# Two token tiles of a fp32 transformer kernel run one after the other across each norm

## The chip, the cores and the metric

The kernel runs on one core of a Trainium2 chip. The metric is the device time of one execution in microseconds (us). One profiled execution gives the trace from which every row below is taken.

## What is computed

Two two-layer blocks follow each other on 256 tokens of width 1024, all in float32. Only the row of operations matters here:

```
for l in 0, 1:   x = x + gate1 * attention(modulate(rmsnorm(x)))      # 88 weight units
                 x = x + gate2 * (relu(h @ w_ff1)^2 @ w_ff2)          # h = modulate(rmsnorm(x)), 64 units
x = rmsnorm(x)
x = layer_norm(ALPHA * x + retention(x))
x = layer_norm(ALPHA * x + swiglu(x))
x = layer_norm(ALPHA * x + sparse_attention(x))
x = layer_norm(ALPHA * x + mixture_of_8_experts(x))
```

Seven norms stand between two stages of matrix products (four RMS norms after the first one, and three layer norms); one more stands before the first product and one after the last.

## The kernel before

**Tiles and units.** The 256 tokens are two tiles of 128 (`NT`). Weights stream through the core in units of 512 KB (128 partitions x 1024 values: two row blocks of 512 columns, or four of 256). For each unit SyncE starts a DMA into `raw` (ring of 4), ScalarE copies it rounded into `whi` (L1175), VectorE writes the rest into `wlo` (L1635), and TensorE multiplies: `unit` (L432) runs both token tiles over one unit, high part with high and low part of the tokens (L440), then the low part of the weights (L446). `whi` and `wlo` are rings of 4, and ScalarE and VectorE split three units ahead (`LEAD`); a slot is free again when `unit_used` has been raised by the last product of its unit. Every unit is 24 products of 128 x 256 or 12 of 128 x 352 or 128 x 512.

**Order.** Each engine's program is written out by hand and waits on counted semaphores. `chunk` and `side_chunk` are four units that sum into one pair of PSUM banks; `side_chunk` leaves the reading of the banks to `c.pending`, which runs after the next split. `pass_units(e, n)` on ScalarE and VectorE is n splits. `c.weave` hangs side work on a unit number.

**Around a norm.** TensorE finishes the last unit of both tiles; VectorE reads the sums out of PSUM and adds them to `x` (L2073 and L2076 after attention, L2089 and L2100 after the MLP, L2160 after retention and SwiGLU, L2331 after sparse attention); the norm's statistics are squares on ScalarE (L1266) or `bn_stats` on VectorE (L2129), then a root on ScalarE (L1257, L1269); VectorE writes the normed tiles (L1776, L2145 and L2148), and drains (L1747, `to_pe`) to release TensorE. TensorE turns tile 0 and tile 1 (`turn_tiles`, L471), eight 128 x 128 blocks each, ScalarE copies each bank of four into `xh` (L1229), VectorE the rest into `xl` (L1714). Only when all four banks are done do the units of the next stage begin. In the MLPs `clear_sums` (L789) stands before them.

## Time and profile before

| | |
|---|---|
| median of three runs | 3045.28 us (3038.07 to 3046.09) |
| the profiled execution | 3036.44 us |
| its span, first to last instruction | 3034.7 us |
| busy: TensorE, VectorE, ScalarE | 2702.1, 2147.5, 1611.3 us |
| mean granted TensorE clock | 0.942 of 2.4 GHz |
| chain that ended last | TensorE 80%, VectorE 8%, ScalarE 5% |
| one 512 KB weight load, issue to landing (medians by tensor) | 4.3 to 5.6 us |
| first matrix product of the experts' routing | 1948.14 us after the start |

The span is the row of stages laid end to end. The seven norms' turns start at 429.4, 643.6, 1015.8, 1226.3, 1467.9, 1684.0 and 1935.8 us. "Idle" is time of one engine before an instruction, with what ended it; PEclk is the granted clock, where 1.00 is 2.4 GHz and 0.50 is 1.2 GHz.

### The profile page before, as it was taken

The numbers are of one execution on the slowest core, as the hardware profiler recorded it, in microseconds if no ns is written. First come the engines' busy times: TensorE is split into PE (matmuls) and PEld (weight loads), VectorE is DVE, ScalarE is ACT, GpSimd is POOL, SyncE is SP. The second block draws the span as 40 slices with busy tenths as digits, with TensorE's granted clock in tenths as the row PEclk, the third lists the DMA queues.
The fourth block names the chain that finished last, engine by engine and source line by source line (L and its number), as shares of the span: only waits on it lengthen the run. The fifth ranks groups of instructions, "written<-read, shape, count | busy, mean of one in ns | idle before, by whom it ended". The sixth has DMA issues, their size and how long they took to land.

```text
span 3034.7 us, 39536 instructions
## 1 busy us (share of the span) xinstructions
PE 2702.1 (89%) x12842; PEld 2183.6 (72%) x12842; DVE 2147.5 (71%) x2585; ACT 1611.3 (53%) x2056; POOL 19.8 (1%) x37
## 2 busy tenths in 40 slices
PE   3889879987988899898899868699999999999997
PEld 2767758875766687666799646578878887888875
DVE  6666657766666565655555675489888998989998
ACT  2454534445454344333344344277767776777775
POOL 0000000000000000000000000000000000000000
PEclk9999989999999899899899868699999999999999
DMA  6636547745464465544455430299989998999995
GB/s 225 202 117 190 172 152 257 250 149 161 133 194 159 141 213 175 176 128 146 142 180 182 129 101 1 79 322 364 338 306 342 330 368 294 361 335 342 358 355 214
DMA packets 357975, 666.19 MB, mean 220 GB/s; under 512 B 23008, under 2 KB 57312, under 8 KB 357200
## 3 DMA queue, kind: packets, MB, share of 16 engines
q1 hardware_dynamic: 354080, 648.45, 63.6%
q0 software_dynamic: 3760, 15.91, 1.6%
q8 instruction: 88, 1.44, 0.2%
q14 instruction: 47, 0.39, 0.0%
HBM read 663.23 MB, written 1.05 MB: 219 GB/s over the span
## 4 chain that ended last, share of the span: by engine, by line
PE 80%; DVE 8%; ACT 5%; issue 3%; DMA 2%; DVEq 2%; ACTq 0%; SPq 0%
PE ps L440 46%; PE ps L446 23%; PE ps L482 2%; DVE wlo L1635 2%; ACT whi L1175 2%; PE ps L1078 1%; DVE mod_sum L1655 1%; DMA raw<-in_w_ada 1%; PE ps L471 1%; PE ps L581 1%; PE ps L516 1%; DMA raw<-in_w_in 1%; ACT att L1334 0%; PE ps L691 0%; DVE yl L1721 0%
## 5 line engine op out<-in xcount | busy, mean ns | idle before, releaser
L1635 DVE TENSOR_TENSOR wlo<-raw,whi 128x1024 fp32r<-128x1024 f32 x709 | 865.8, 1224 | 582.4 <-ACT whi L1175 576.1
L1175 ACT ACTIVATE whi<-raw 128x1024 fp32r<-128x1024 f32 x709 | 749.1, 1060 | 794.5 <-PE ps L446 679.0
L440 PE MATMUL ps<-whi,xh 128*128 128x512 f32 (+3 forms) x1376 | 512.2, 382 | 19.4 <-issue 6.1
L440 PE MATMUL ps<-whi,xl 128*128 128x512 f32 (+3 forms) x1376 | 496.5, 371 | 0.0
L440 PE MATMUL ps<-whi,gathered_hi 128*128 128x512 f32 x896 | 362.9, 405 | 16.9 <-issue 11.2
L440 PE MATMUL ps<-whi,gathered_lo 128*128 128x512 f32 x896 | 356.1, 397 | 0.0
L446 PE MATMUL ps<-wlo,xh 128*128 128x512 f32 (+3 forms) x1376 | 326.1, 365 | 0.0
L440 PEld LDWEIGHTS ps<-whi,xh 128*128 128x128 f32 x1376 | 270.9, 197 | 72.4 <-issue 15.4
L440 PEld LDWEIGHTS ps<-whi,xl 128*128 128x128 f32 x1376 | 271.3, 197 | 43.3 <-issue 4.0
L440 PE MATMUL ps<-whi,yh 128*128 128x512 f32 (+2 forms) x696 | 280.7, 405 | 20.8 <-DVE yl L1721 11.6
L446 PE MATMUL ps<-wlo,gathered_hi 128*128 128x512 f32 x896 | 283.1, 397 | 0.0
L440 PE MATMUL ps<-whi,yl 128*128 128x512 f32 (+2 forms) x696 | 273.8, 395 | 0.0
L446 PEld LDWEIGHTS ps<-wlo,xh 128*128 128x128 f32 x1376 | 242.0, 194 | 42.1
L1635 DVE TENSOR_TENSOR wlo<-spare,whi 128x1024 fp32r<-128x1024 f32 x168 | 204.5, 1224 | 19.0 <-ACT whi L1175 17.4
L1635 DVE TENSOR_TENSOR wlo<-mod_b,whi 128x1024 fp32r<-128x1024 f32 x168 | 205.4, 1222 | 16.2 <-ACT whi L1175 11.3
L440 PEld LDWEIGHTS ps<-whi,gathered_hi 128*128 128x128 f32 x896 | 169.7, 189 | 56.8 <-issue 16.8
L1175 ACT ACTIVATE whi<-spare 128x1024 fp32r<-128x1024 f32 x168 | 178.9, 1065 | 52.1 <-PE ps L446 52.1
L1175 ACT ACTIVATE whi<-mod_b 128x1024 fp32r<-128x1024 f32 x168 | 178.3, 1061 | 49.8 <-PE ps L446 49.5
L446 PEld LDWEIGHTS ps<-wlo,gathered_hi 128*128 128x128 f32 x896 | 169.3, 189 | 41.3
L440 PEld LDWEIGHTS ps<-whi,gathered_lo 128*128 128x128 f32 x896 | 169.8, 190 | 37.0
L446 PE MATMUL ps<-wlo,yh 128*128 128x512 f32 (+2 forms) x696 | 189.7, 393 | 5.9 <-DVE wlo L1635 5.9
L440 PE MATMUL ps<-whi,hidden_hi 128*128 128x512 f32 x448 | 178.5, 398 | 2.5 <-DVE hidden_lo L1721 1.3
(358 smaller groups left out, 3305.6 us busy)
## 6 DMA issues: line engine op xcount, KB each, us to landing
raw<-in_moe_w_in SPq DMA_DIRECT2D x227, 512.0 KB, 5.4
spare<-in_moe_w_in SPq DMA_DIRECT2D x165, 512.0 KB, 5.6
mod_b<-in_moe_w_out SPq DMA_DIRECT2D x165, 512.0 KB, 5.5
raw<-in_w_ff SPq DMA_DIRECT2D x128, 512.0 KB, 4.5
raw<-in_w_ada SPq DMA_DIRECT2D x96, 512.0 KB, 4.3
raw<-in_w_in SPq DMA_DIRECT2D x96, 512.0 KB, 4.5
work<-in_moe_w_in SPq DMA_DIRECT2D x56, 512.0 KB, 5.4
work<-in_moe_w_out SPq DMA_DIRECT2D x56, 512.0 KB, 5.2
```

What stands on the lines that cost most here:

```text
L440: e.matmul(ps[0:lhs[2], banks[t], at:at + width], part[:, k0 + j, t * P:t * P + lhs[2]], whi[:, slot, w], start=first and j == 0 and part ...
L446: mm = e.matmul(ps[0:lhs[2], banks[t], at:at + width], lhs[0][:, k0 + j, t * P:t * P + lhs[2]], wlo[:, slot, w], start=False, stop=last an ...
L471: tr = e.transpose(ps[:, bank, j * P:(j + 1) * P], src(t, b + j), ident)
L482: tr = e.transpose(ps[:, bank, (j * tiles + t) * P:(j * tiles + t + 1) * P], src(t, b + j), ident)
L516: e.matmul(ps[:, 7, :], k_("ones"), mod_sum[:, n % 2, :], start=True, stop=True).then_inc(mod_summed, 1)
L581: mm = e.matmul(ps[:, 4 + t, h * HD:(h + 1) * HD], side_pT[g][:, at:at + P], v(b, h), start=b == 0, stop=b == t)
L1078: mm = e.matmul(ps[:, bank, j * P:(j + 1) * P], part[:, t, k * P:(k + 1) * P], onehot[b][:, t, :], start=t == 0, stop=t == 1)
L1175: e.activation(whi[:, slot, :], src, ACT.Copy).then_inc(split_hi, 1)
L1635: e.tensor_tensor(wlo[:, slot, :], src, whi[:, slot, :].bitcast(F32), ALU.subtract).then_inc(split_lo, 1)
L1655: last = e.scalar_tensor_tensor(total, w[:, j, :], c_col[:, k:k + 1], total, ALU.mult, ALU.add)
```

## The change

The last four units before a norm (two after SwiGLU) and the first four units after it are run tile by tile: `by_tile` runs tile 0 through all units of the group and then tile 1, so all four ring slots hold their units until tile 1 has used them. `tile_used` tells VectorE when tile 0's columns are summed. The output units of the last MLP step and of retention are ordered by column half, and SyncE's loads with them. VectorE reads, norms and hands over tile 0, splits a unit, and then does the same for tile 1; the low-part copies of the turned tiles (`turn_first`, `turn_second`) stand among the splits. TensorE turns tile 0 before the next group and tile 1 before the group's fourth unit of tile 0. Wide operations become pieces of 512 columns of one tile. ScalarE runs a small root (`ready_root`) early, squares each tile by halves, and roots each tile by itself. `clear_sums` comes after the first four units. Side work of the modulation in the MLP moves one unit earlier, `scale_gain` two. At the kernel's start the first chunk alone is run by tile. After the sparse attention only the last four units are, since the routing follows the norm. The last layer norm is as before.

```diff
+            def half_unit(e, lhs, t, ahead, k0, bank, width, first, last, blocks=UROWS, at=0):
+
+                slot, _ = c.slot(ahead)
+                e.wait_ge(split_hi, c.at("unit", ahead + 1))
+                for j in range(blocks):
+                    w = slice(j * USIZE // blocks, j * USIZE // blocks + width)
+                    for part in lhs[:2]:
+                        e.matmul(ps[:, bank, at:at + width], part[:, k0 + j, t * P:(t + 1) * P], whi[:, slot, w],
+                                 start=first and j == 0 and part is lhs[0], stop=False)
+                e.wait_ge(split_lo, c.at("unit", ahead + RING + 1))
+                for j in range(blocks):
+                    w = slice(j * USIZE // blocks, j * USIZE // blocks + width)
+                    mm = e.matmul(ps[:, bank, at:at + width], lhs[0][:, k0 + j, t * P:(t + 1) * P], wlo[:, slot, w],
+                                  start=False, stop=last and j == blocks - 1)
+                return mm
+
+            def by_tile(e, lhs, group, between={}, tell=False):
+
+                for t in range(NT):
+                    for i, (k0, banks, width, first, last, blocks, at) in enumerate(group):
+                        for piece in between.get((t, i), ()):
+                            piece(e)
+                        mm = half_unit(e, lhs, t, i if t == 0 else 0, k0, banks[t], width, first, last, blocks, at)
+                        if t == 0:
+                            if last and tell:
+                                mm.then_inc(tile_used, 1)
+                            continue
+                        mm.then_inc(unit_used, 1)
+                        c.add("unit")
+                        for piece in c.passed():
+                            piece(e)
+
+            def tile_turns(src, t):
+
+                def piece(e):
+                    source(e)
+                    for b in range(0, KB, 4):
+                        bank = 6 + c.parity("t")
+                        e.wait_ge(t_lo, c.at("t", 1))
+                        for j in range(4):
+                            tr = e.transpose(ps[:, bank, j * P:(j + 1) * P], src(t, b + j), ident)
+                        tr.then_inc(t_ready, 1)
+                        c.add("t")
+                return piece
+
+            def from_turns(src, second):
+
+                return {(0, 0): [lambda e: e.wait_ge(t_lo, c.at("t", 1))], (0, second): [turned],
+                        (0, 3): [tile_turns(src, 1)], (1, 0): [turned]}
+
+            def first_chunk(e, src, lhs, width=UCOLS):
+
+                tile_turns(src, 0)(e)
+                side = c.parity("chunk")
+                e.wait_ge(evac_act, c.at("chunk", 1))
+                e.wait_ge(evac_dve, c.at("chunk", 1))
+                by_tile(e, lhs, [(i * UROWS, (2 * side, 2 * side + 1), width, i == 0, i == 3, UROWS, 0) for i in range(4)],
+                        from_turns(src, 2))
+                c.add("chunk")
...
+            def last_out(e, hid, kind):
+
+                n_kg = kind[0] // 256
+                by_tile(e, hid, [(kg * UROWS, (2 + 2 * n, 3 + 2 * n), UCOLS, False, kg == n_kg - 1, UROWS, 0)
+                                 for n in range(2) for kg in range(n_kg)], tell=True)
+
+            def mlp(e, src, lhs, hid, width, kind):
                 wide, _, pair, tiles = kind
                 steps = width // wide
+                tile_turns(src, 0)(e)
+                e.wait_ge(evac_act, c.at("chunk", 1))
+                e.wait_ge(evac_dve, c.at("chunk", 1))
+                if kind is SWIGLU:
+                    group = [(4 * i, (0, 1), wide, i == 0, i == 1, 4, part * wide) for part in range(2) for i in range(2)]
+                else:
+                    group = [(i * UROWS, (0, 1), UCOLS, i == 0, i == 3, UROWS, 0) for i in range(4)]
+                by_tile(e, lhs, group, from_turns(src, 1 if kind is SWIGLU else 2))
...
-                step_out(e, hid, kind, last=True)
+                last_out(e, hid, kind)
...
-                turn_tiles(e, lambda t, b: work[:, t, b * P:(b + 1) * P], KB)
-                turned(e)
-                for _ in range(3):
+                    at(ATT_UNITS - SIDE + 8 * n + 16, sum_modulation)
+
+                first_chunk(e, lambda t, b: work[:, t, b * P:(b + 1) * P], X, 352)
+                for _ in range(2):
...
-                chunk(e, Y, NT, D)
-
-                turn_tiles(e, lambda t, b: work[:, t, b * P:(b + 1) * P], KB)
-                turned(e)
-                mlp(e, X, Y, D_FF, RELU2)
+                last_chunk(e, Y)
+
+                mlp(e, lambda t, b: work[:, t, b * P:(b + 1) * P], X, Y, D_FF, RELU2)
...
+            def layer_norm_roots(e, units):
+
+                pass_units(e, 1)
+                ready_root(e)
+                for t in range(NT):
+                    vec(e)
+                    e.activation(st[:, 8 + t:9 + t], st[:, t:t + 1], ACT.Sqrt).then_inc(act_ready, 1)
+                    if t == 0:
+                        pass_units(e, units - 1)
+                        nothing_to_read(e)
+                        turn(e, xh, KB, by_tile=(0,))
...
+                def last_columns(e, t):
+                    tmp = att[:, 1024 + t * 512:1536 + t * 512]
+                    e.tensor_tensor(tmp, ps[:, 2 * side + t, :], gate1[1], ALU.mult)
+                    e.drain()
+                    if t:
+                        e.sem_inc(evac_dve, 1)
+                        e.sem_inc(bias_used[1], 1)
+                    e.tensor_tensor(x[:, t, 512:D], x[:, t, 512:D], tmp, ALU.add)
+                    to_act(e)
+                pass_units(e, 1)
+                to_act(e)
+                for t in range(NT):
+                    scaled_half(e, mod_a, t, 0)
+                tile_done(e)
+                last_columns(e, 0)
+                scaled_half(e, mod_a, 0, 1)
+                tile_inverse(e, 0)
+                shifted_tile(e, mod_a, 0)
+                pass_units(e, 1)
+                e.wait_ge(unit_used, c.at("unit", RING + 2))
+                last_columns(e, 1)
+                turn_first(e)
+                pass_units(e, 1)
+                scaled_half(e, mod_a, 1, 1)
+                tile_inverse(e, 1)
+                shifted_tile(e, mod_a, 1)
+                pass_units(e, 1)
+                c.add("chunk")
...
+            def add_columns(e, t, n, src):
+
+                w = slice(n * 512, (n + 1) * 512)
+                e.scalar_tensor_tensor(x[:, t, w], x[:, t, w], ALPHA, src, ALU.mult, ALU.add)
+                e.drain()
+                if t and n:
+                    e.sem_inc(evac_dve, 1)
+                e.bn_stats(st[:, 32 + 12 * t + 6 * n:38 + 12 * t + 6 * n], x[:, t, w])
+
+            def tile_deviation(e, t):
+
+                e.drain()
+                e.bn_aggr(st[:, 64 + 2 * t:66 + 2 * t], st[:, 32 + 12 * t:44 + 12 * t])
+                e.drain()
+                e.tensor_scalar(st[:, t:t + 1], st[:, 65 + 2 * t:66 + 2 * t], LN_EPS, None, ALU.add)
+                to_act(e)
+
+            def normed_tile(e, t):
+
+                e.scalar_tensor_tensor(x[:, t, :], x[:, t, :], st[:, 64 + 2 * t:65 + 2 * t], gain_a[:, :],
+                                       ALU.subtract, ALU.mult)
+                tile_inverse(e, t)
+                e.scalar_tensor_tensor(x[:, t, :], x[:, t, :], st[:, 16 + t:17 + t], gain_b[:, :], ALU.mult, ALU.add)
+                to_pe(e)
+
+            def layer_norm_by_tile(e, units, src, done=()):
+
+                pass_units(e, 1)
+                take_gain(e, 0)
+                take_gain(e, 1)
                 for n in range(2):
-                    if n:
-                        half_moments(e, 0)
-                    e.wait_ge(unit_used, c.at("unit", RING - 1 + n))
-                    w = slice(n * 512, (n + 1) * 512)
-                    for t in range(NT):
-                        e.scalar_tensor_tensor(x[:, t, w], x[:, t, w], ALPHA, ps[:, 2 + 2 * n + t, :], ALU.mult, ALU.add)
-                e.drain().then_inc(evac_dve, 1)
+                    if n not in done:
+                        tile_done(e)
+                        add_columns(e, 0, n, src(0, n))
+                tile_deviation(e, 0)
+                normed_tile(e, 0)
+                if 0 not in done:
+                    e.wait_ge(unit_used, c.at("unit", RING + units // 2 - 1))
+                    add_columns(e, 1, 0, src(1, 0))
+                pass_units(e, 1)
+                turn_first(e)
+                e.wait_ge(unit_used, c.at("unit", RING + units - 2))
+                add_columns(e, 1, 1, src(1, 1))
+                tile_deviation(e, 1)
+                if units > 2:
+                    pass_units(e, 1)
+                normed_tile(e, 1)
+                if units > 2:
+                    pass_units(e, 1)
+                c.add("chunk")
+                e.sem_inc(gain_a_used, 1)
+                e.sem_inc(gain_b_used, 1)
...
-            def mlp_out(e, w_out, kind, s):
-                for kg in range(kind[0] // 256):
-                    for n in range(2):
-                        (load_expert if kind is EXPERT else load)(
-                            e, rows(w_out, s * kind[0] + kg * 256)[:, :, n * 512:(n + 1) * 512])
+            def mlp_out(e, w_out, kind, s, by_columns=False):
+                order = [(kg, n) for kg in range(kind[0] // 256) for n in range(2)]
+                for kg, n in sorted(order, key=lambda o: o[::-1]) if by_columns else order:
+                    (load_expert if kind is EXPERT else load)(
...
-            for kg in range(8):
-                for n in range(2):
-                    load(sp, rows(a["ret_w_out_2"][0], kg * 256)[:, :, n * 512:(n + 1) * 512])
+            for kg, n in [(kg, n) for kg in range(6) for n in range(2)] + [(kg, n) for n in range(2) for kg in (6, 7)]:
+                load(sp, rows(a["ret_w_out_2"][0], kg * 256)[:, :, n * 512:(n + 1) * 512])
```

## Rows read from the trace of the kernel before

**Rows 1.** Waits of TensorE: us in total, times, longest.

```profile
PE ps L471 <- DVEq L1747: 69.7, 8, 11.5
PE ps L471 <- DVE xl L1714: 8.8, 8, 1.9
```

**Rows 2.** Windows over seven passages: busy (x) by engine, PEclk, DMA share, GB/s.

```profile
409.70:450.62 40.92, 30.47 (x117) 22.94 (x115) 22.73 (x24) 14.64 (x18) 1.60 (x3) 0.79 0.40 129
623.35:659.16 35.81, 24.85 (x112) 21.56 (x113) 22.96 (x24) 12.36 (x17) 0.53 (x1) 0.81 0.27 76
996.17:1037.36 41.19, 30.74 (x117) 23.13 (x115) 22.72 (x24) 14.64 (x18) 0.00 (x0) 0.79 0.30 103
1206.69:1245.79 39.10, 28.87 (x112) 22.87 (x113) 20.24 (x21) 12.35 (x17) 2.09 (x4) 0.78 0.48 164
1447.59:1491.13 43.54, 31.23 (x165) 26.57 (x163) 23.27 (x28) 12.25 (x14) 5.69 (x7) 0.76 0.43 124
1669.32:1703.99 34.67, 22.62 (x89) 17.92 (x90) 20.72 (x26) 9.23 (x12) 1.06 (x2) 0.75 0.27 85
1917.85:1948.14 30.29, 15.26 (x65) 11.98 (x64) 20.76 (x24) 10.29 (x12) 1.06 (x2) 0.76 0.16 52
```

**Rows 3.** Windows inside the first passage, same columns.

```profile
421.00:429.40 8.40, 0.02 (x1) 0.03 (x1) 6.32 (x7) 3.88 (x6) 1.60 (x3) 0.73 0.61 196
429.40:442.20 12.80, 10.73 (x32) 7.46 (x33) 5.28 (x6) 3.34 (x5) 0.00 (x0) 0.51 0.14 43
```

**Rows 4.** Timeline of TensorE, first passage: start, us, operation, [idle before].

```profile
429.38 1.97 PE L471 MATMUL ps<-const,work 128*128 128x128 f32 x8 [8.38 <-DVEq L1747]
...
437.17 0.80 PE L440 MATMUL ps<-whi,xh 128*128 128x512 f32 x1
```

**Rows 5.** Timeline of TensorE: unit pace at 352 and 256 columns; four turns.

```profile
655.36 0.32 PE L440 MATMUL ps<-whi,xh 128*128 128x352 f32 x1
...
657.26 0.32 PE L440 MATMUL ps<-whi,xh 128*128 128x352 f32 x1
...
1485.43 0.28 PE L440 MATMUL ps<-whi,xh 128*128 128x256 f32 x1
...
1488.28 0.28 PE L440 MATMUL ps<-whi,xh 128*128 128x256 f32 x1
...
1498.81 0.60 PE L482 MATMUL ps<-const,att 128*128 128x128 f32 x4
```

**Rows 6.** Timeline of VectorE, first passage.

```profile
411.05 1.23 DVE L1635 TENSOR_TENSOR wlo<-raw,whi 128x1024 fp32r<-128x1024 f32 x1 [1.56 <-ACT whi L1175]
...
421.04 1.29 DVE L2073 TENSOR_TENSOR att<-ps,mod_a 128x512 f32<-128x512 f32 x2 [0.40 <-PE ps L446]
...
428.01 2.69 DVE L1776 SCALAR_TENSOR_TENSOR work<-work,st,mod_a 128x1024 f32<-128x1024 f32 x2
431.16 0.69 DVE L1714 TENSOR_TENSOR xl<-ps,xh 128x512 fp32r<-128x512 f32 x1 [0.46 <-ACT xh L1229]
```

**Rows 7.** Timeline of ScalarE, first passage.

```profile
423.71 1.06 ACT L1266 ACTIVATE att<-x 128x1024 f32<-128x1024 f32 x1 [4.32 <-DVEq L1740]
...
430.53 0.60 ACT L1229 ACTIVATE xh<-ps 128x512 fp32r<-128x512 f32 x1 [2.80 <-PE ps L471]
```

**Rows 8.** Timeline of VectorE at the layer norm after retention.

```profile
1458.68 1.28 DVE L2160 SCALAR_TENSOR_TENSOR x<-x,ps 128x512 f32<-128x512 f32 x2
1460.05 1.29 DVE L2129 BATCH_NORM_STATS2 st<-x 128x6 f32<-128x512 f32 x2
...
1465.20 1.28 DVE L2145 SCALAR_TENSOR_TENSOR x<-x,st,gain_a 128x1024 f32<-128x1024 f32 x1 [0.16 <-issue]
```

**Rows 9.** Windows after short idles in the two attention layers.

```profile
262.00:272.00 10.00, 6.29 (x25) 4.67 (x24) 7.25 (x11) 6.19 (x13) 0.00 (x0) 0.83 0.55 168
...
848.00:858.00 10.00, 6.28 (x33) 5.17 (x34) 6.71 (x9) 7.29 (x15) 0.00 (x0) 1.00 0.66 205
```

**Rows 10.** Window over the experts' stage.

```profile
1948.14:3034.70 1086.56, 1041.04 (x4658) 834.09 (x4658) 945.75 (x989) 790.71 (x882) 0.00 (x0) 0.97 0.92 326
```

More of the change, by code:

```diff
@@ L1487, in retention @@
                 root(e, 8)
-                for half in range(2):
-                    turn(e, yh, KB)
-                    pass_units(e, 8)
-                c.add("chunk")
-                left_to_dve(e)
-                root(e, 2)
+                turn(e, yh, KB)
+                pass_units(e, 8)
+                turn(e, yh, KB)
+                pass_units(e, 4)
+                layer_norm_roots(e, 4)
             def sparse_attention(e):
-                turn(e, xh, KB, by_tile=True)
                 for i in (3, 4):
-                    chunk(e, D, copy_to(proj[:, 0, i * 512:(i + 1) * 512]))
+                    chunk(e, D, copy_to(proj[:, 0, i * 512:(i + 1) * 512]), {0: [turn_second]} if i == 3 else {})
                 def gates(e, b):
@@ L1920, in mlp @@
                 turn(e, hid[0], hid[1], kind[0] // P, kind[3])
-                pass_units(e, kind[0] // P)
-                c.add("chunk")
+                end(e)
             def layer(e, l):
@@ new lines, in from_mlp @@
+                    turn_first(e)
+                    e.wait_ge(unit_used, c.at("unit", RING + 2))
+                    columns(1, 1)
+                    pass_units(e, 1)
+                    if l + 1 < DEPTH:
+                        for n in range(2):
+                            scaled_half(e, mod_b, 1, n)
+                    normed(1)
+                    if l + 1 == DEPTH:
+                        e.sem_inc(gain_a_used, 1)
+                    pass_units(e, 1)
+                    c.add("chunk")
@@ L2112, in inverse_deviation, with tile_done @@
+                mlp(e, (yh, yl), D_FF, RELU2, from_mlp)
+            def tile_done(e):
+                c.add("tile")
+                e.wait_ge(tile_used, c.at("tile"))
             def inverse_deviation(e, n, final=False):
@@ L2229, in retention @@
                         to_pe(e)
-                for half in range(2):
-                    turn(e, yh, yl, KB)
-                    pass_units(e, 8)
-                c.add("chunk")
+                turn(e, yh, yl, KB)
+                pass_units(e, 8)
+                turn(e, yh, yl, KB)
+                pass_units(e, 4)
                 e.drain().then_inc(extra_used, 1)
-                add_mlp(e)
-                layer_norm(e)
+                layer_norm_by_tile(e, 4, mlp_sum)
             def act_copied(e):
```

298 lines of the change are left out of this document (165 added, 133 removed).

## The prediction

> **What bounds the kernel now.** I read the table of busy times and the chain first: TensorE is the engine that ends last nearly everywhere. Then TensorE's waits: the largest is not for weights but for VectorE's drain ahead of the turns at the norms, 69.7 us in 8 places, of which 11.5 us is the kernel's start, so 58.2 us in seven norms; 8.8 us more goes while the turned tiles are copied [rows 1]. Third, the windows. I cut a passage around each norm, from the first product of the last group of units before it to the last product of the first four units after it; for the seventh, to the first product of the routing [rows 2]. The six full passages last 40.9, 35.8, 41.2, 39.1, 43.5 and 34.7 us, the seventh 30.3. Their DMA share is 0.16 to 0.48, so weights are not what they wait for. Fourth, the inside of the first passage: 8.4 us with TensorE idle and VectorE busy for 6.3, and behind it 12.8 us at a granted clock of 0.51, the lower level of 1.2 GHz [rows 3]: turns, cleared sums and a first unit that starts at 437.17, 16.2 us after the last product [rows 4]. The time is lost twice, as a gap and as slow work behind it.
>
> **The floor of a passage.** A unit of 512 columns takes 2.79 us (passage one begins with four of them in 11.3 us, before the window of 8.4 us idle [rows 2, 3]); 352 columns take 1.90 and the 256-column form 2.85 [rows 5]. Four turns take about 0.45 us start to start at the full clock (0.60 with the tail [rows 5]), sixteen about 1.9. So the first passage holds 8 x 2.79 + 1.9 + 0.9 (cleared sums at the full clock) = 25.1 us of TensorE work in 40.9. I don't expect the floor: VectorE has its own chain.
>
> **The change, walked through.** Prices on VectorE: a split 1.23, a 512-column read or add 0.69 alone and 0.64 in a pair, a scaled and shifted tile 1.35, a low copy 0.69 [rows 6]; a 1024-column layer-norm pass 1.28, a statistics piece 0.69 alone [rows 8]. On ScalarE: a split 1.06, a bank of the turned tile 0.60, a 1024-column square 1.06 and so a half about 0.6 plus 0.2 to read its sum [rows 7]. A drain or a hand-off is counted at 0.1 to 0.3.
>
> First passage, microseconds from its start. TensorE runs tile 0 until 5.6 and tile 1 until 11.2, at no new cost: the same 48 products. The fourth unit's low part is ready at 2.6 and is needed at about 5. VectorE reads the earlier columns until 5.1, scales two halves until 6.4, reads and adds tile 0's last columns until 7.9, scales until 8.6; square and root end on ScalarE at 9.2; the inverse and the shifted tile are done at 11.0, before TensorE is free. Tile 0 costs TensorE nothing: its whole norm lies under tile 1's products. Then the order of VectorE decides. A split (12.2), tile 1's last columns (13.6), tile 0's two low copies (14.3, 14.9), a split (16.2), scaling, inverse and shift of tile 1 (18.5), a split (19.7), a split (20.9), then tile 1's low copies. TensorE turns tile 0 at 11.2 to 12.1, waits to 14.4, runs the half of unit one, waits 0 to 0.5 us in unit two, waits in unit three for the low part of 19.7 (about 1.6 us), turns tile 1 until 21.1, runs unit four's half until 22.5, waits 0.4 for tile 1's copies, and runs tile 1's four halves to 28.5; cleared sums bring 29.4. That is 11.5 less than 40.9.
>
> The others, in the same way. Passage two (MLP to 352-column chunk): both column halves of tile 0 are read in turn as `tile_used` rises, VectorE's fourth split comes at about 21.9, tile 1's pass starts at 24.0 and takes 3.8: 27.8 against 35.8, 8.0 less. Passage three as one: 11.8. Passage four (final RMS norm, 512 columns, no cleared sums): 28.9 against 39.1, 10.2. Passage five (layer norm, 256 columns): tile 0's two statistics pieces and two passes end at 10.7, tile 1's at 21.0, splits three and four at 22.3 and 23.5, tile 1's pass from 25.6 to 31.3, cleared sums 32.3 against 43.5: 11.2. Passage six has only two units ahead of the norm (5.6 us of cover for a chain of 8), ends at 25.9 against 34.7: 8.8. Passage seven gains only what tile 0's norm hides, since routing needs both tiles: 28.0 against 30.3, 2.3. The sum is 11.5 + 8.0 + 11.8 + 10.2 + 11.2 + 8.8 + 2.3 = 63.8 us.
>
> At nothing I count: the start (turns of tile 1 slip behind three half units, but its copies wait as long as before; bounds -1 and +1); the reordered loads (same bytes, and the DMA share in the passages leaves room [rows 2]; without that cover a load landing late would cost up to the 4.3 to 5.6 us that one load takes from issue to landing, by the table above); the modulation's sums one unit earlier, which move on TensorE and VectorE together; `ready_root`, which lies in ScalarE's wait of 4.3 us [rows 7]; the narrow pieces' extra fixed cost, already in the prices for single pieces. A slot held for both tiles is queued before the next splits on ScalarE and, behind them, on VectorE: unit five's split can start only when tile 1 has used unit one, at 24.3 in passage one, and is whole at 26.6 where TensorE asks at 28.5, so 1.9 us of slack cover it.
>
> **What the walk leaves out.** Two things. Hand-offs: the walk has some fifteen per passage and lets them overlap ideally; between 0 and 2 us a passage, I take 1, so 6 us. The clock: TensorE now has several idles of 0.4 to 2.3 us within some 12 us. Near such a cluster the trace shows both outcomes: idles of 1.4 and 2.3 us at 264 and 267 us with a granted clock of 0.83 in that window, and idles of 3.0 and 1.8 us at the same place of layer two with 1.00 [rows 9]. If it falls, tile turns and half units run at half pace. Waits for VectorE swallow part of that, the tail does not: for passage one I get about 34 instead of 29.4, so 5 us a passage, 30 in six. The bounds are 0 and 30; rows 9 are one and one, so I take half, 15.
>
> The Trainium skill, page "TensorE: Matmul & The Clock Gate", section "A second HAM failure mode: psum-queue depth-cycling", says that short idles between groups of products, if frequent enough, make the clock swing between its levels even where no single idle is long. By that rule all six passages would fall, and the sum would be lower by the other 15 us. The trace agrees in one of the two places compared.
>
> The forecast is 63.8 - 6 - 15 = 43 us. The profiled execution of 3036.4 us would become 2993.5; its run lay 9 us under the median of 3045.3, so I forecast a median of 3002 us.
>
> **The rivals.**
> Everything fits: clock held at 2.4 GHz, hand-offs hidden. Gain 64, time 2981. For it: every single idle in the walk is under 3 us, as in the window at 848 us with clock 1.00. Against it: up to 5 us of waits in some 12 us, in passage two more than 7.
> The clock falls in every passage: 63.8 - 6 - 30 = 28, time 3017. For it, and by the rule of that page: passages two and five have the most idle. Against it: the work between the idles is dense.
> No change that can be told: the tile-1 chain on VectorE is later than walked, by 7 us more in each passage, through another order of splits and copies than I read. VectorE's busy time in a passage is 20.2 to 23.3 us [rows 2], so even a chain with no overlap at all would end a passage near 23 plus a pass of 4 to 6; that is under all lengths but leaves 5 to 12. Time about 3040.
> Slower: the low clock begins at the first idle and lasts beyond the passage. Each us of products at 1.2 GHz that would have run at 2.4 loses half of it. Before, the first passage shows 12.8 us of it [rows 3]. From about 9.5 us lost per passage (57.8/6), so 19 us of unbroken low clock, the gain is gone; at 24 us of it the kernel is about 15 us slower, 3060. Against it: the clock came back within 5 us of dense work at 437.17.
> Could the experts swallow it? Their stage has a DMA share of 0.92 [rows 10], but it holds none of the changed passages, and its loads beyond the first three wait for the routing, which comes earlier with all else; it is only moved.
>
> **How the numbers follow.** Chances: forecast (a gain of 32 to 56 us) 0.55, everything fits 0.17, clock falls everywhere 0.20, no change 0.04, slower 0.04. About 0.3%, 9 us, is what a measurement of this kernel can tell from no change; faster is thus 0.93, same 0.03, slower 0.04. The range takes in both clock bounds with some us of the run-to-run spread: 2979 to 3024. Range of the likeliest alone: 2989 to 3013.
>
> **What would show it.** The wait of L471 for VectorE's drain falls from 69.7 us to under 20, nearly all of it the kernel's start. The six passages last 28 to 34 us. In them VectorE is busy without a gap of 1 us from tile 0's first read to tile 1's low copies; new waits of TensorE are for `wlo` (in the half of unit two or three) and for `xl`. Cleared sums at 0.9 us show a held clock, at 1.9 a fallen one. Wrong would be: TensorE waiting for the split of unit five (the slots), the turn of tile 0 waiting for VectorE by more than 2 us in passages one to five, or a granted clock below 0.6 over a whole new passage.

## The result: 77 us faster, 37 us more than forecast

| | before | after |
|---|---|---|
| median | 3041.76 us (3038.07 to 3046.09, 4 runs) | 2964.83 us (2963.28 to 2965.93, 4 runs) |
| profiled execution, its span | 3036.44, 3034.7 us | 2964.59, 2962.7 us |
| mean granted TensorE clock | 0.942 | 0.954 |

The ratio is 0.9744, with a 95% interval of 0.9731 to 0.9757. The forecast was 3002 us with a range of 2979 to 3024: the sign was right, and the time lies 14 us below the range.

The span shrank by 72.0 us. I cut the span after at the same places as [rows 2] and [rows 10]. Windows of the kernel after: length, busy time (and count) of TensorE, its weight loads, VectorE, ScalarE and GpSimd, then granted clock, DMA share, GB/s.

```profile
409.35:439.05 29.70, 27.15 (x117) 20.96 (x115) 22.42 (x27) 16.61 (x28) 1.61 (x3) 0.94 0.50 157
613.39:642.90 29.51, 23.88 (x112) 20.75 (x113) 20.95 (x27) 12.89 (x25) 0.00 (x0) 0.88 0.25 73
978.78:1008.84 30.06, 27.14 (x117) 20.85 (x115) 22.45 (x27) 16.62 (x28) 0.00 (x0) 0.94 0.36 121
1179.82:1208.60 28.78, 25.23 (x113) 19.60 (x114) 19.22 (x23) 12.32 (x24) 2.10 (x4) 1.00 0.48 160
1413.94:1445.79 31.85, 26.37 (x165) 22.55 (x163) 23.32 (x30) 11.93 (x16) 5.71 (x7) 1.00 0.55 150
1625.49:1652.47 26.98, 22.02 (x89) 17.22 (x89) 19.91 (x28) 9.31 (x14) 1.06 (x2) 0.87 0.33 110
1866.15:1894.39 28.24, 14.15 (x66) 11.39 (x64) 21.09 (x27) 10.36 (x14) 1.06 (x2) 0.78 0.17 57
1894.39:2962.70 1068.31, 1036.90 (x4658) 832.52 (x4658) 945.28 (x989) 790.33 (x882) 0.00 (x0) 0.98 0.93 331
```

| stretch | before, us | after, us | gain |
|---|---|---|---|
| start to the first passage | 409.70 | 409.35 | 0.35 |
| the seven passages | 265.52 | 205.12 | 60.4 |
| the six stretches between them | 1272.92 | 1279.92 | -7.0 |
| routing to the end | 1086.56 | 1068.31 | 18.25 |

Two readings. In the first passage VectorE does as much work as before (22.42 us against 22.94) and ScalarE 2 us more (16.61 against 14.64), but TensorE's share of the time rose: it is busy for 27.15 of 29.70 us, against 30.47 of 40.92, part of which was slow work. And the last row, a stage that the change doesn't touch, gave a quarter of the gain.

TensorE's waits in the kernel after (us in total, times, longest), against 69.7 and 8.8 us in [rows 1]:

```profile
PE ps L461 <- DVE xl L1833: 15.0, 13, 2.7
PE ps L494 <- DVEq L1866: 13.8, 2, 11.5
PE ps L466 <- DVE wlo L1754: 9.2, 6, 2.7
PE ps L541 <- DVEq L1866: 7.5, 1, 7.5
```

L461 and L466 are the products of half units, L494 the turns. Of the 13.8 us, 11.5 is the kernel's start; the 7.5 us is the seventh norm, where both tiles must be there. So 58.2 us of waiting for a norm became 9.8, and waits for the low copies (`xl`) and for the splits (`wlo`) are now the longer ones. TensorE in the first passage of the kernel after (start, duration, [idle before]), with `...` where lines are left out:

```profile
420.52 1.04 PE L494 MATMUL ps<-const,work 128*128 128x128 f32 x8
423.93 0.47 PE L461 MATMUL ps<-whi,xh 128*128 128x512 f32 x1 [2.38 <-DVE xl L1833]
424.24 0.39 PE L461 MATMUL ps<-whi,xl 128*128 128x512 f32 x1
...
424.80 0.63 PE L461 MATMUL ps<-whi,xl 128*128 128x512 f32 x1
...
428.35 0.40 PE L461 MATMUL ps<-whi,xh 128*128 128x512 f32 x1
...
429.74 1.03 PE L494 MATMUL ps<-const,work 128*128 128x128 f32 x8
...
432.35 0.50 PE L461 MATMUL ps<-whi,xh 128*128 128x512 f32 x1 [0.17 <-DVE xl L1833]
...
438.12 1.03 PE L859 MATMUL ps<-zero 1*128 1x512 bf16 x4
```

The turns start as the last product ends, where [rows 4] had 8.38 us of idle. The clock does fall behind the 2.38 us of idle: a 512-column product takes 0.63 in place of 0.39 us from 424.80 on. From 424.24 to 428.35 us the granted clock is 0.58, from there to the passage's end it is 1.00, and the cleared sums at 1.03 us agree. VectorE in the same passage, which the walk had laid out step by step:

```profile
415.78 0.68 DVE L2209 TENSOR_TENSOR att<-ps,mod_a 128x512 f32<-128x512 f32 x1
...
418.72 1.28 DVE L1902 SCALAR_TENSOR_TENSOR work<-work,st,mod_a 128x1024 f32<-128x1024 f32 x1
420.13 1.23 DVE L1754 TENSOR_TENSOR wlo<-raw,whi 128x1024 fp32r<-128x1024 f32 x1
...
422.98 1.29 DVE L1833 TENSOR_TENSOR xl<-ps,xh 128x512 fp32r<-128x512 f32 x2
...
426.16 1.28 DVE L1902 SCALAR_TENSOR_TENSOR work<-work,st,mod_a 128x1024 f32<-128x1024 f32 x1
427.56 2.36 DVE L1754 TENSOR_TENSOR wlo<-raw,whi 128x1024 fp32r<-128x1024 f32 x2
```

Counted from 409.35, tile 0's shifted tile ends at 10.7 us (walk: 11.0), its low copies at 14.9 (14.9), tile 1's shifted tile at 18.1 (18.5), the last two splits at 20.6 (20.9).

**Where the 18 us come from.** Behind the routing stands a loop over two experts at a time. Its body runs three times, so TensorE jumps back to its start twice. TensorE in the kernel before, at both back-jumps, and windows behind them:

```profile
2248.11 0.79 PE L440 MATMUL ps<-whi,gathered_hi 128*128 128x512 f32 x1 [3.11 <-issue]
...
2253.57 0.79 PE L440 MATMUL ps<-whi,gathered_hi 128*128 128x512 f32 x1 [4.24 <-issue]
...
2512.35 0.50 PE L440 MATMUL ps<-whi,gathered_hi 128*128 128x512 f32 x1 [2.38 <-ACT whi L1175]
...
2516.93 0.80 PE L440 MATMUL ps<-whi,gathered_hi 128*128 128x512 f32 x1 [3.85 <-issue]
```

```profile
2248.00:2266.00 18.00, 13.64 (x49) 10.53 (x50) 7.98 (x10) 6.91 (x8) 0.00 (x0) 0.73 0.55 185
2512.00:2530.00 18.00, 13.80 (x53) 10.84 (x54) 9.84 (x12) 7.29 (x9) 0.00 (x0) 0.81 0.62 207
```

TensorE stands still twice at each back-jump. In three of the four stalls it waits for nothing that the profile shows ("issue"); the one of 2.38 us is put down to ScalarE's split, but no kernel without stalls waits there. A low clock follows. That is 13.6 us of idle and the slow work behind it. The kernel after, 3 us behind the first product after its first back-jump (2191.74):

```profile
2195.00:2213.00 18.00, 18.00 (x81) 13.98 (x79) 17.45 (x24) 12.46 (x14) 0.00 (x0) 1.00 0.97 351
```

That is 81 products where the kernel before ran 49. One more row differs, the instruction queue (packets, MB, share of 16 engines), first before, then after:

```profile
q8 instruction: 88, 1.44, 0.2%
```

```profile
q8 instruction: 70, 1.15, 0.2%
```

A packet is 16 KB (1.44 MB in 88), which is 256 instructions of the 64 bytes that each takes in the compiled program. Counted in the programs as built, with a weight load for each product, TensorE's instructions ahead of this loop number 13996 before and 14016 after; the body has 1598 in both. The compiler adds some: in its file for TensorE the loop starts at instruction 15058 before and 15078 after, and the body has 1601. The shift of 20 is the same. The places modulo 256 that the expectations give (172 and 192) are by the first count; in the file each is 38 higher.

The traces hold the start of every packet of this queue, and they show what the stalls are. Elsewhere one packet starts each time TensorE goes from one block of 256 instructions to the next. The kernel before starts a packet at 2240.1 us, jumps back at 2242.4, and then loads eight more in that pass, at 2245.3, 2251.2 and 2256.6 us and on to 2432.1; in the last pass it does the same, from 2504.0 on. The kernel after starts none between 2184.5 and 2718.2 us: both its jumps go to instructions that it still holds.

### The profile page after: what moved, and what is told of

The parts are those of the page before. It is cut to its first block, busy times and chain, and to the rows that moved or that the text cites. A ratio compares the mean times of both kernels' runs of the same rounds, so it can differ in the third digit from the quotient of the medians.

```text
span 2962.7 us, 39672 instructions
## 1 busy us (share of the span) xinstructions
PE 2690.2 (91%) x12842; PEld 2175.1 (73%) x12842; DVE 2148.3 (73%) x2610; ACT 1614.2 (54%) x2094; POOL 19.8 (1%) x37
## 4 chain that ended last, share of the span: by engine, by line
PE 79%; DVE 9%; ACT 5%; issue 3%; DVEq 2%; DMA 2%; ACTq 0%; SPq 0%
PE ps L441 44%; PE ps L447 21%; DVE wlo L1754 2%; PE ps L552 2%; PE ps L461 2%; ACT whi L1250 2%; PE ps L1153 1%; PE ps L466 1%; DVE mod_sum L1774 1%; DMA raw<-in_w_in 1%; DMA raw<-in_w_ada 1%; PE ps L586 1%; PE ps L651 1%; ACT att L1463 0%; PE ps L761 0%
## 5 line engine op out<-in xcount | busy, mean ns | idle before, releaser
L441 PE MATMUL ps<-whi,xh 128*128 128x512 f32 (+2 forms) x1248 | 463.5, 382 | 13.6 <-issue 6.1
L441 PE MATMUL ps<-whi,xl 128*128 128x512 f32 (+2 forms) x1248 | 448.0, 369 | 0.0
L447 PE MATMUL ps<-wlo,xh 128*128 128x512 f32 (+2 forms) x1248 | 295.2, 364 | 0.0
L441 PEld LDWEIGHTS ps<-whi,xh 128*128 128x128 f32 x1248 | 242.7, 195 | 60.5 <-issue 13.4
L441 PEld LDWEIGHTS ps<-whi,xl 128*128 128x128 f32 x1248 | 243.3, 195 | 40.4 <-issue 4.4
L441 PE MATMUL ps<-whi,yh 128*128 128x512 f32 (+2 forms) x592 | 241.3, 409 | 15.6 <-DVE yl L1840 7.1
L447 PEld LDWEIGHTS ps<-wlo,xh 128*128 128x128 f32 x1248 | 218.1, 193 | 39.1
L441 PE MATMUL ps<-whi,yl 128*128 128x512 f32 (+2 forms) x592 | 233.4, 396 | 0.0
L1754 DVE TENSOR_TENSOR wlo<-mod_b,whi 128x1024 fp32r<-128x1024 f32 x168 | 205.4, 1222 | 15.9 <-ACT whi L1250 11.0
L441 PEld LDWEIGHTS ps<-whi,gathered_lo 128*128 128x128 f32 x896 | 169.2, 189 | 37.1
L441 PE MATMUL ps<-whi,hidden_lo 128*128 128x512 f32 x448 | 177.0, 395 | 0.0
```

Of the source, the lines that this page charges most:

```text
L441: e.matmul(ps[0:lhs[2], banks[t], at:at + width], part[:, k0 + j, t * P:t * P + lhs[2]], whi[:, slot, w], start=first and j == 0 and part ...
L447: mm = e.matmul(ps[0:lhs[2], banks[t], at:at + width], lhs[0][:, k0 + j, t * P:t * P + lhs[2]], wlo[:, slot, w], start=False, stop=last an ...
L1754: e.tensor_tensor(wlo[:, slot, :], src, whi[:, slot, :].bitcast(F32), ALU.subtract).then_inc(split_lo, 1)
```

## The experiments

The kernel before was timed again beside the experiments, in three sets with medians of 3039.21, 3040.86 and 3039.82 us (11, 9 and 9 runs); ratios are against the same set. Differences to the kernel after are against its 2964.83 us, which was measured apart.

### Is it the place of the loop?

The first theory: the 18 us belong to the 20 instructions that TensorE's program grew by, not to the norms. The rival: they come from the earlier or denser stage ahead. Both kernels were moved by increments of a semaphore that nobody waits for:

```diff
+            for _ in range(20):          # in the kernel after: 236, 256, 128 and 200
+                pe.sem_inc(pe_tick, 1)
             pe.wait_ge(const_ready, 16)
```

> The kernel before with 20 semaphore increments at the head of TensorE's program, where it waits 22 us anyway; it computes the same. They move its later instructions by 20 places, to where the changed kernel has them. Placement theory (the experts' loop over two experts fetches its instructions anew on each pass before the change and not after, because the changed program is 20 instructions longer ahead of it): the experts' stage falls from 1086.6 to about 1068 us, instruction loads from 9 per pass to none, the whole by 18 to 23 us to about 3020. Rival (the stage is faster because of what runs ahead of it, the norm by tile and the earlier loads): no change, about 3041.

Measured: 3020.16 us (3017.44 to 3028.71), ratio 0.9943 (0.9929 to 0.9956). Routing to end 1067.8 us, no stall at the back-jumps, 70 packets.

> The changed kernel with 236 increments at the same place, which puts the loop where the kernel before has it if instructions are fetched in blocks of 256 (the 16 KB of one load, at 64 bytes each). Placement theory: the experts' stage is back near 1086 us, the whole near 2983, with instruction loads on each pass again. Rival: no change, 2965.

Measured: 2994.12 us (2992.53 to 2996.59), ratio 0.9855 (0.9841 to 0.9869), 29.3 us more than the kernel after. Routing to end 1088.4 us, 20.1 more, and 89 packets; the other 9 us are lost at the start, to the increments themselves. The four stalls are back; the kernel after with 236 increments, TensorE:

```profile
2202.38 0.49 PE L441 MATMUL ps<-whi,gathered_hi 128*128 128x512 f32 x1 [2.65 <-ACT whi L1252]
...
2207.02 0.79 PE L441 MATMUL ps<-whi,gathered_hi 128*128 128x512 f32 x1 [3.91 <-issue]
...
2466.15 0.49 PE L441 MATMUL ps<-whi,gathered_hi 128*128 128x512 f32 x1 [3.05 <-issue]
...
2471.30 0.80 PE L441 MATMUL ps<-whi,gathered_hi 128*128 128x512 f32 x1 [4.36 <-issue]
```

> The changed kernel with 256 increments: a whole block, so the loop stands in its block as in the changed kernel. Placement theory: 2965, no change, although more is added than in the run with 236. Rival (added instructions cost by their number): at least as slow as the run with 236. The increments themselves lie in the first 22 us of waiting and should cost nothing.

Measured: 2977.18 us (2974.42 to 2979.24), ratio 0.9795 (0.9783 to 0.9808). Routing to end 1067.5 us, 71 packets, no stall. The total missed, since the increments were taken to be free: TensorE's first turn came at 70.71 us in place of 57.79. These 12.9 us are the whole difference to the kernel after (12.4).

So the loop's place alone takes 19.1 us off the kernel before, and alone adds 20 us to the kernel after. The rival (the earlier or denser stage ahead) fell. A second set asked which places stall:

> The kernel after with 128 increments of a semaphore at TensorE's start, which nobody waits for. The increments themselves cost 0.05 us each by the runs with 236 and 256, so 6.4 us. Theory of blocks: TensorE's instructions come in blocks of 256 (packets of 16 KB on the instruction queue); the body of the loop over two experts is 1598 instructions long and touches seven blocks from most starts, eight from 62 starts in 256; only a body that touches eight is loaded anew in each pass. The starts seen so far (counted modulo 256 as the program has them: 172 stalls, twice; 192 doesn't, three times) put the stalling starts at about 112..131 to 172..191. This one stands at 64: no stalls, router to end 1067 to 1069 us, 70 or 71 packets, 2971 us. Rival (a start below that of the kernel after, by any number, is bad, since what matters is the distance to one place): stalls, 2992 us, 88 packets.

Measured: 2965.17 us (2964.0 to 2966.2), ratio 0.975 (0.9735 to 0.9765). 71 packets, no stall, routing to end 1070.2 us. First turn at 57.51 us: these increments cost nothing, against 6.4 us expected, and so the total came out 6 us below the expected 2971.

> The kernel after with 200 such increments: 10 us of their own. Its loop starts at 136 modulo 256. Theory of blocks: inside the stalling starts, so 88 or 89 packets, four stalls of 2 to 4.5 us at the two back-jumps, router to end 1086 to 1089 us, 2993 to 2996 us. Rival (the stalls belong to the one start at 172, where a certain instruction falls on an edge): none here, 2975 us.

Measured: 2976.36 us (2967.44 to 2977.28), ratio 0.9779 (0.9763 to 0.9795). 89 packets, as the theory of blocks said, but routing to end 1078.5 us and 2976 in place of 2993 to 2996, since only two of the four stalls are there. One of its four executions took 2967.44 us, 8 less than the next; no trace shows why. The kernel after with 200 increments, TensorE:

```profile
2197.95 0.50 PE L441 MATMUL ps<-whi,gathered_hi 128*128 128x512 f32 x1 [3.81 <-issue]
...
2457.22 0.49 PE L441 MATMUL ps<-whi,gathered_hi 128*128 128x512 f32 x1 [2.84 <-ACT whi L1252]
```

Seven kernels (these five, before and after) sort by the place of the loop's start modulo 256. Starts at 136 and 172 have 88 or 89 packets and stalls; starts at 64 and 192 have 70 or 71 and none. The five kernels of the sections below keep the start at 192, and all have 70 packets.

**Where the blocks' edges lie.** In the kernel before and in the one with 236 increments, the second stall of each jump comes after two products, 8 instructions behind the loop's start in the compiled file. There TensorE crosses into the next block. Taking the edge to be there, the distance from the loop's start to the next edge follows for all seven: 8 instructions (before, and 236 increments), 44 (200), 116 (128) and 244 (after, 256 increments, and the kernel before with 20). The body of 1601 is six blocks and 65 instructions, so it lies in eight blocks where the distance is under 65 and in seven otherwise. That is just how the kernels sort. It also accounts for the count of stalls: with a distance of 8 TensorE stalls for the block it jumps to and at once for the next, while with 44 there is no second idle: the next packet starts at 2200.2 us, beside the products behind 2197.95. Near its end the body has one block more loaded, the one behind it (the packets at 2240.1 and 2184.5 us). Seven blocks and this one are kept; eight and this one are not, and then all eight are loaded anew, nine packets a pass with the one behind.

The Trainium skill, page "Runtime: NRT & Kernel Launch", section "Instruction fetch mechanics", says that TensorE holds 2048 instructions, refilled in 16 KiB blocks of 256. The packets agree (16 KB each), and so does the sorting, once the block behind the body is counted: eight blocks of 256 stay, nine don't. The same section says that a taken branch out of a window of two blocks stalls; here, jumps back over six blocks ran without a stall where the packets weren't repeated, so the measurement decides against that sentence.

### What each half of the reordering is worth

The kernel after has two covers: tile 1's products of the group ahead hide tile 0's norm, tile 0's products of the group behind hide tile 1's. Each was undone on TensorE alone, with the length of its program ahead of the loop kept at the kernel after's; the order of VectorE and ScalarE stayed, so what that order is worth by itself under TensorE's new order isn't measured.

```diff
 def first_chunk(...):                       # and the same in mlp
                 tile_turns(src, 0)(e)
+                tile_turns(src, 1)(e)
+                turned(e)
...
-                by_tile(e, lhs, [(i * UROWS, ...) for i in range(4)], from_turns(src, 2))
+                for i in range(4):
+                    unit(e, lhs, NT, i * UROWS, (2 * side, 2 * side + 1), width, i == 0, i == 3)
```

> The changed kernel, but the first group of units behind each norm is run unit by unit as before the change, after both tiles are turned; VectorE and ScalarE are as in the changed kernel (14 increments at the head keep the loop's place). The groups ahead of the norms stay tile by tile. Theory (both sides of the change give time): by the walk tile 1's products then start about where tile 1's pass starts now, and all eight halves follow instead of four, so each of six passages is 3 to 6 us longer: 2985 to 2995. Rival (the whole gain comes from tile 0's norm under tile 1's products, and VectorE's chain sets the end behind the norm): no change, 2965.

Measured: 2990.04 us (2989.64 to 2993.03), ratio 0.9842 (0.9828 to 0.9856): 25.2 us more than the kernel after, within the expected range. The six passages grew by 2.9 to 6.7 us, 35 in all, and the stretches between them shrank by 10.5. Routing to end 1068.5 us.

```diff
 def by_tile(...):
-                for t in range(NT):
-                    for i, (...) in enumerate(group):
+                order = [(t, i) for t in range(NT) for i in range(len(group))]
+                if tell:                    # the groups ahead of a norm
+                    order = sorted(order, key=lambda o: o[::-1])
+                for t, i in order:
...
```

> The kernel after with the last four units ahead of each norm run unit by unit again (both token tiles of a unit, then the next), so the first tile's sums are whole only one half unit before the second's; the first four units behind each norm stay tile by tile. The number of TensorE's instructions ahead of the loop over two experts is that of the kernel after. My theory (the earlier first tile lets VectorE and ScalarE norm it under the second tile's products): the wait between the last product ahead and the first product behind grows from about 2.4 us by the 5 half units that no longer cover the norm, 4 to 5.6 us, in the passages of four units, less in the sixth with its two: 3 to 5 us per passage, 20 to 32 us in all with the lower clock behind each wait, so 2985 to 2997 us. Rival: it is the products behind alone that hide the norm (the runs of the kernel with those unit by unit cost 25 us of the 60 that the passages gave); then this one costs under 8 us, below 2973. The experts' stage stays at 1067 to 1069 us in both.

Measured: 2991.1 us (2987.62 to 2991.72), ratio 0.9834 (0.9819 to 0.9849): 26.3 us more, within the expected range as well. The passages with a group of four ahead of the norm grew by 3.3 to 4.4 us, the sixth by 0.8. Routing to end 1070.0 us.

> The kernel after with TensorE running both groups unit by unit, the last four units ahead of each norm and the first four behind it, while VectorE and ScalarE keep the order, the pieces and the hand-offs of the kernel after. The number of TensorE's instructions ahead of the loop over two experts is that of the kernel after. Undoing the group behind alone cost 25 us, the group ahead alone 26 us. If the two covers are separate (one hides tile 0's norm, the other tile 1's), both undone cost about 51 us: 3016 us, close to the kernel before with its loop moved by 20 instructions (3020), and the other edits (pieces of a tile, early root, turns first and then cleared sums) are worth 0 to 8 us together. Rival: undone together they cost clearly more or less than the sum, since with both gone the lower clock covers the whole passage (3025 or more) or since the waits of the one lay in those of the other (3000 or less). Router to end 1067 to 1070 us in all cases.

Measured: 3020.62 us (3017.46 to 3024.84), ratio 0.9941 (0.9925 to 0.9957): 55.8 us more than the kernel after, against 51.5 for the sum of the two: it lies between the expected 3016 and the rival's 3025. TensorE's waits in this kernel begin with nearly the time of [rows 1] (69.7 us), in more pieces since each tile is turned by itself:

```profile
PE ps L497 <- DVEq L1876: 72.8, 13, 11.5
```

This kernel is as fast as the kernel before with its loop moved (3020.16). It has all the pieces, early roots and copies of the kernel after, so those give nothing that can be told without TensorE's order. The two steps, 19.1 us for the place of the loop and 55.8 for the order, make 74.9 of the 76.9 us.

### The early root

The small root of `ready_root` was left out; nobody reads its result.

> The kernel after without the small root that ScalarE runs early in each passage (left out: a root of a constant that nobody reads). The table load of 1.28 us, seen at 410.76 us under the products ahead in the first passage, then stands ahead of tile 0's root. Tile 0's normed tile is ready there about when TensorE comes free, so the load reaches the wait behind the turns: 0.5 to 1.2 us in each of the four to seven passages that load the table, 3 to 8 us in all, 2968 to 2973 us. Rival: the load stays hidden (tile 0's chain has 1.3 us of slack), 2965 us.

Measured: 2966.09 us (2962.65 to 2972.58), ratio 0.9766 (0.9751 to 0.9782), the same as the kernel after. ScalarE in the first passage, first in the kernel after, then without the root:

```profile
410.76 1.28 ACT L1350 ACT_TABLE_LOAD   x1
412.06 0.20 ACT L1350 ACTIVATE st<-const 128x1 f32<-128x1 f32 x1
...
418.15 0.29 ACT L1366 ACTIVATE st<-st 128x1 f32<-128x1 f32 x1
```

```profile
418.29 1.28 ACT L1366 ACT_TABLE_LOAD   x1
419.58 0.30 ACT L1366 ACTIVATE st<-st 128x1 f32<-128x1 f32 x1
```

The table load did move ahead of tile 0's root, and the first passage grew by about 1 us (to the cleared sums: 28.77 to 29.73). In the total nothing is left of it that could be told from the spread of 10 us. The expectation of 3 to 8 us was wrong, and its rival (2965) held.

### A better place for the second tile's turns

In the kernel after TensorE waits for the low part of the fourth unit and turns tile 1 only then. The experiment turns tile 1 one unit earlier:

```diff
-                return {(0, 0): [...], (0, second): [turned],
-                        (0, 3): [tile_turns(src, 1)], (1, 0): [turned]}
+                pieces = {(0, 0): [...], (0, second): [turned], (1, 0): [turned]}
+                pieces.setdefault((0, 2), []).append(tile_turns(src, 1))
+                return pieces
```

> The kernel after with the second tile's eight turns ahead of the third unit of the first tile's products in place of the fourth, and 6 increments at the start so that the loop over two experts starts where it does in the kernel after (0.3 us). In the passages where the lower part of the fourth unit is late (2.73 us at 634.40, 2.31 us at 1435.77) the turns, 1 us, and the splits behind them come under that wait; my theory gives 0.5 to 1 us in each of five passages, 2 to 4 us in all, so 2961 to 2963 us. Rival: the second tile's norm isn't done by then (VectorE's last instruction of it ends at 633.00 in the second passage, the third unit's products start at 628.31... 630.85), so the turns block the products that could run before it, and the wait only moves ahead: 2965 to 2972 us.

Measured: 2956.02 us (2954.09 to 2961.86, 5 runs), ratio 0.9727 (0.9713 to 0.974). In the same set the kernel after with 128 free increments took 2965.17 us (2964.0 to 2966.2), so it is 9 us faster, against 2 to 4 expected. TensorE in the second passage, first the kernel after, then this one:

```profile
630.42 0.59 PE L466 MATMUL ps<-wlo,xh 128*128 128x352 f32 x2 [1.31 <-DVE wlo L1754]
...
634.40 0.96 PE L466 MATMUL ps<-wlo,xh 128*128 128x352 f32 x2 [2.73 <-DVE wlo L1754]
635.16 1.91 PE L494 MATMUL ps<-const,work 128*128 128x128 f32 x8
```

```profile
629.43 0.59 PE L466 MATMUL ps<-wlo,xh 128*128 128x352 f32 x2 [1.25 <-DVE wlo L1757]
632.15 1.94 PE L494 MATMUL ps<-const,work 128*128 128x128 f32 x8 [2.13 <-issue]
```

The turns do wait, by 2.13 us, as the rival said; over the kernel their waits grew by 5.4 us. But the waits for `wlo` in half units fell from 9.2 us in 6 places to 1.8 in 2, and those for `xl` from 15.0 to 12.6. That VectorE's last splits now lie under the turns is the likely reason; it wasn't tested apart. Five of the six passages became 0.6 to 1.8 us shorter and the third 0.8 longer, 4.1 us in all. The profiled executions differ by 10.5 us, and most of the rest lies where the edit changes nothing: 3.8 us between the sixth and the seventh passage, where nearly the same number of products (982 and 981) kept TensorE busy for 171.3 us at a granted clock of 0.82 in the kernel after and for 164.6 at 0.85 here. So the edit is shown to be worth about 4 us; whether the rest is its doing stays open.

## Why the prediction missed

**The step that failed** is the sentence on the experts: "it holds none of the changed passages [...] it is only moved". Their stage became 18.25 us shorter. I had looked for what an earlier start could do to its loads, and had not asked what a longer program does to a loop behind it, though the rows were there before the change: 11.2 us of "issue" ahead of `gathered_hi` in the table of groups, and 88 packets on the instruction queue. What the runs showed in its place: the 20 instructions that TensorE's program grew by move the loop so that its body lies in seven blocks of 256 in place of eight, 18 packets and four stalls go, and this is worth 19.1 us in the kernel before (20 idle instructions added) and 20 us in the kernel after (236 added).

**The walk of the passages** was right in its mechanism and close in its size. It gave 63.8 us; measured are 60.4. By passage: 11.2 (walk 11.5), 6.3 (8.0), 11.1 (11.8), 10.3 (10.2), 11.7 (11.2), 7.7 (8.8), 2.05 (2.3). The run with both halves undone agrees: together they are worth 55.8 us.

**The two discounts**, 6 for hand-offs and 15 for the clock, were terms of the sum that came out too large: together by 10.6 us. In the passages only 3.4 us were lost; 7.0 more were lost between them. The clock behaved as neither bound said: it fell in part, with windows of 0.94, 0.88, 0.94, 1.00, 1.00 and 0.87, and in the first for 4 us and not to the passage's end. The half that the prediction took had weak support: of the two idles that the prediction names in layer two, only the one of 3.0 us (at 849.90) stands at the same product as one in layer one (2.3 us, at 266.98). The other two (1.8 and 1.4 us) have no partner in the other layer, so the two windows of [rows 9] are not one case with two outcomes. The rule of the Trainium skill that the prediction weighed ("TensorE: Matmul & The Clock Gate", section "A second HAM failure mode: psum-queue depth-cycling") would have made it fall in all six; two held the full clock, passage five with 5.5 us of idle in it.

**Between the passages** 7.0 us were lost that the walk didn't have. In the stretches behind the first, third and fifth passages the loss comes with the group behind run by tile. From product to product they last 172.6, 169.2 and 178.0 us before and 174.2, 170.9 and 179.6 after; 175.4, 170.8 and 179.6 where only the group ahead was undone; but 171.8, 168.3 and 177.1 where the group behind was. That is 1.6 us each, some 5 in all. The 3.5 us in the stretch with retention (clock 0.97 to 0.95) seem to be this one execution's: in five other traces of kernels with the same order on TensorE it lasts 201.8 to 202.3 us, as before (201.9), and not 205.4, while their fifth passage is 1.2 us longer. Part of the loss is the clock. Behind the first passage the same kind of idle, 2.55 us before and 2.61 after, was followed by a window of clock 1.00 before and of 0.72 after. What decides between them no run tells.

**The starting point.** 8.8 us of the miss is the difference between the profiled execution (3036.44) and the median of three (3045.28) that I added. The kernel before spreads over 8 us from run to run, and its later medians were 3039 to 3042, midway between the two. So about half of the 8.8 was luck of the three runs. In all: 18.25 + 10.95 (42.8 forecast against 53.75 outside the experts' stage) + 8.8 = 38 us, for a miss of 37. Without the experts' stage the time would have been about 2983 us, inside the range.

**The rest.** The order of the new waits came as told: `xl`, then `wlo`; the wait for the norm ahead of the turns is 13.8 us, nearly all the start. Tile 0's turn waited 2.23 us in the sixth passage, as its shorter cover had it, and nowhere else. The slots held for tile 1 cost little at most: at its first unit behind passages one, three and five TensorE waits 2.61, 2.59 and 1.77 us, against 2.55, 2.55 and 1.73 before; with the group behind undone these waits are 1.0 us shorter each. `ready_root` at nothing was right, and stays right without it.

**Open:** what decides whether the clock falls behind an idle of 2.5 us; whether the fast stretch in the run with earlier turns belongs to the edit.

## What to carry to other kernels

Two tiles that pass a norm one after the other hide it twice: the second tile's products ahead cover the first tile's norm, and the first tile's products behind cover the second's. Each half was worth about 25 us here, and both together 56, slightly more than their sum. A walk of one passage with durations from the trace of before came within 0.1 to 1.7 us in each of seven; discount it little, and check the parts that "are only moved": a program that changes length ahead of a long loop can gain or lose time that has nothing to do with the edit, 19 to 20 us of 3000 here. Before an effect is put down to an edit, pad the old kernel to the new one's length and run it.

## What was not expected of the hardware

- A loop body of 1601 TensorE instructions ran without any stall where it lay in seven blocks of 256. Where it lay in eight (20 instructions away) 9 packets of 16 KB were loaded again in each of two passes, with stalls of 2.4 to 4.4 us at the back-jump. In the kernel before, the clock in the 18 us behind it was 0.73 and 0.81. The price in the experts' stage was 19 to 20 us with two stalls a jump, and about 10 with one (200 increments).
- The block edge's distance from the loop's start decided the number of stalls: 8 instructions gave two at each jump, 44 gave one.
- Semaphore increments at the start of TensorE's program: the first 128 cost nothing (first turn at 57.51 us against 57.79), since the first product waits for other work anyway; from 200 to 256 the first turn moves from 62.06 to 70.71 us, 0.155 us each.
- The clock came back from its lower level within 4 us of dense half units in the first passage (424.80 to 428.35).
